# Gate stage of a hybrid Mamba-2 / S5 block: turning a group's x to tokens by VectorE block transposes and a trip through DRAM, in place of TensorE transposes

## Chip, cores and metric

One core of one Trainium2 chip runs the kernel. The metric is the device time of one execution in microseconds, lower is better.

## What is computed

The reference is a decoder block on 256 tokens with model width 2048, all in float32. One product of the normed input with `w_in` gives z, x, B, C, dt, the S5 input u and two gate vectors. The change is in the Mamba-2 mixer:

```
xbc = silu(causal_dwconv(xbc, conv_w, conv_b));  xs, bm, cm = split(xbc)
dt  = softplus(dt_raw + dt_bias)                      # (tokens, 48 heads)
xh  = xs as (tokens, 8 groups, 6 heads, 64)
y   = ssd_chunked(xh * dt_g, dt_g * a, bm, cm)        # one chunk of 256 tokens
      # cb = C B^T;  y_diag = (cb * decay) (xh * dt)
y   = (y + d_skip * xh) * silu(z); group norm; @ w_proj
```

The merged mixers then go through `w_out`, a residual, and a gated feed-forward part.

## The kernel before

Activations lie channel-major: 128 channels on the partitions, 256 tokens along the free dimension. Every weight matrix arrives in **units** of 128 x 1024 floats (512 KB). SyncE loads a unit into one of four ring slots of `raw`, ScalarE copies it to `whi` in the fp32r format (`split_hi`, L666), VectorE writes the rest `raw - whi` to `wlo` (`split_lo`, L1107), and TensorE multiplies both. Unit n's slot is loaded again once unit n has been split, and unit n+4 is split by ScalarE once TensorE has used unit n.

Each engine runs a program of its own, in the order of the code, with waits on semaphores. Nothing is scheduled by a tool: if an instruction waits, everything written behind it on that engine waits too.

The stages follow each other: u, zx (z and x, six turns), bc (B and C, two turns), gate, proj, glu, out, up, down. The **gate stage** has eight turns, one for each group of heads. Turn i multiplies the eight gate units 8i to 8i+7 (numbered 0 to 7 in the turn; I write "turn 1, unit 5") and does the attention-like part of group i between them:

- GpSimd broadcasts the decay rows of a group to all partitions, three heads a DMA (`load_decay`, L442, tile `dec`). The rows of group i+1 are asked for when TensorE's products of group i have read the buffer (`y_ready`).
- VectorE runs three scans over each half of `dec` (L1416), ScalarE takes the exponential (L853).
- TensorE computes CB = B^T C (L1924, L1925) and turns the group's three 128 x 256 tiles of x to token-major with six 128 x 128 transposes against an identity (L1933, into `XP` in PSUM). It reads copies that ScalarE has made into fixed buffers (`bst`, L856, and `xst`, L857).
- VectorE masks CB (L1428), multiplies the transposed x by dt from PSUM into `xtok` (L1433, twice), and multiplies `dec` by CB (L1422, one for each half).
- TensorE forms the heads' outputs (L1908, L1909: "heads(0)", "heads(1)").
- VectorE adds the skip term (L1478) and multiplies by silu(z) (L1481); ScalarE squares (L895); the group norm follows in the next turn.

In ScalarE's program a turn ends: split of unit 6's successor, square, the last split (`hi(7)`, which is unit 3 of the next turn), copy of the finished gate chunk out of PSUM (L899), and then the next turn's `hi(0)`, which is unit 4 of that turn. In VectorE's program turn 1 has a special order: `lo(0)` (unit 4 of turn 1), the six scans of both halves, `lo(1)` (unit 5 of turn 1), and then the mask and the decay products. In later turns the first three scans are already done at the end of the turn before. In turn 0 the heads come after all eight units, in turn 1 after unit 5, in later turns after unit 4.

Of the kernel before, what the change touches and what calls it, by code (L numbers as in the profile page):

```python
# [26 lines left out]
ds = bass.ds  # L27

P = 128
# [79 lines left out]
def build_program(nc, a, out):  # L109
    ctx = ExitStack()  # L110
    with ctx:
# [53 lines left out]
        xst = at("xst", [P, TPG, L], F32, W + 9216)  # L165
# [22 lines left out]
        bst = at("bst", [P, L], F32, C + 2048)  # L188
# [11 lines left out]
        merged_at = nc.dram_tensor("merged_blocks", (2, 4, 32, 4, 128), F32).ap()  # L200
        blocks_at = nc.dram_tensor("up_blocks", (4, 32, 4, 256), F32).ap()
# [4 lines left out]
        CB, XP = psum[:, 4, 0:ML], [psum[:, 5, 0:ML], psum[:, 6, 0:ML]]  # L206
# [7 lines left out]
        def sem(name):  # L214
# [32 lines left out]
        z_done, conv_done, xbc_done, staged, cb_ready, xp_ready, scan_ready, exp_ready, m_ready, y_ready = map(  # L247
            sem, ("z_done", "conv_done", "xbc_done", "staged", "cb_ready", "xp_ready", "scan_ready", "exp_ready",
                  "m_ready", "y_ready"))
        half_hi, half_lo = sem("half_hi"), sem("half_lo")  # L250
        ns_free, late_sum, late_h = map(sem, ("ns_free", "late_sum", "late_h"))
# [44 lines left out]
        def _(sp):  # L296
# [39 lines left out]

            for c in range(4):
# [10 lines left out]
            for name in list(PHASES)[1:]:  # L348
                groups, quads, per = PHASES[name]
                if name == "zx":  # L350

                    sp.dma_start(parm[:, KT:], a["parm"][:, KT:]).then_inc(parm_rest, 16)
                    sp.dma_start(craw[:, :, :, :], a["s5_c"]).then_inc(c_in, 16)
                if name == "up":
# [68 lines left out]
        def _(pool):  # L423
# [198 lines left out]
            with pool.Fori(0, GROUPS - 1) as i:  # L622
# [33 lines left out]
        def _(act):  # L656
# [107 lines left out]
            def group_tap(name, i, r):  # L764
# [5 lines left out]
                act.nop(nofuse=True)  # L770
                for t in range(2):
# [72 lines left out]
            def gate_turn(i, prev, last=False):  # L844
# [10 lines left out]
                def stage(g):  # L855
                    fn(bst[:, :], bc[:, ds(g, 1), 0, :].rearrange("p o n -> p (o n)"), ACTF.Copy).then_inc(staged, 1)  # L856
                    fn(xst[:, :, :], zx[:, ds(g * TPG, TPG), 1, :], ACTF.Copy).then_inc(staged, 1)  # L857

                if prev is None:
# [5 lines left out]
                    act.wait_ge(xbc_done, 16)  # L865
                    stage(0)
# [7 lines left out]
                    hi(3)  # L874
                    decay(1)
# [20 lines left out]
                hi(7)  # L896

# [201 lines left out]
        def _(dve):  # L1099
# [287 lines left out]
            with dve.Fori(1, 6) as i:  # L1387
                step.enter(i, 4 * 3 + 2 * 5, 1)
                mixer_turn("zx", i, i, ("zx", i - 1, 3))
                step.leave(6)  # L1390
            mixer_turn("bc", 0, 6, ("zx", 5, 3))
# [14 lines left out]
            def gate_turn(i, prev, first_scan=False, next_scan=True):  # L1406
# [19 lines left out]
                def tokens():  # L1426
                    dve.wait_ge(cb_ready, i + 1)
                    V.tensor_tensor(cbm[:, :], CB, mask_in[:, :], ALU.mult)  # L1428
                    dve.wait_ge(xp_ready, i + 1)
                    if prev is None:  # L1430
                        step.done(V.tensor_copy(dtt[:, :, :], DTT))
                    for k in range(2):
                        ins = V.tensor_tensor(  # L1433
                            xtok[:, k, :].rearrange("p (h n) -> p h n", h=HPG),
                            XP[k].rearrange("p (h n) -> p h n", h=HPG),
                            dtt[:, k, ds(i * HPG, HPG)].rearrange("p (h o) -> p h o", o=1).to_broadcast([P, HPG, 64]),
                            ALU.mult)
                    step.done(ins)

                if prev is None:  # L1440
# [9 lines left out]
                    tokens()  # L1450
                    blocks(0)
                    blocks(1)
                else:
# [6 lines left out]
                    tokens()  # L1460
# [8 lines left out]
                lo(4)  # L1469
                lo(5)  # L1470
# [282 lines left out]
        def _(pe):  # L1753
# [356 lines left out]
```

## Time and profile before

| what | value |
|---|---|
| median of 3 runs | 1680.87 us (1680.24 to 1680.9) |
| the profiled execution | 1680.3 us, span of its instructions 1678.6 us |
| TensorE busy | 1667.1 us, 99% |
| VectorE, ScalarE, GpSimd busy | 1320.3, 962.7, 216.4 us |
| DMA traffic | 358.49 MB, mean 214 GB/s |
| gate stage | from about 431 to 644 us of the span |

TensorE has hardly any idle time, so the time is the sum of its work as long as the other engines deliver each unit before TensorE reaches it. An engine that is less busy matters only where it hands something over late.

### The profile page before, as it was taken

The page shows a single profiled execution, that of the slowest core. Times are in us where ns is not written, and L with a number is a line of the kernel's source. Part 1 is how long each engine was busy: PE and PEld are TensorE (multiplying, and loading weights), DVE is VectorE, ACT ScalarE, POOL GpSimd, SP SyncE. Part 2 cuts the span into 40 slices and gives each one's busy share as a digit, 9 for nine tenths or more (in the row PEclk, how much of TensorE's full clock was granted, in tenths as well). Part 3 has the DMA queues.
Part 4 walks back from the last instruction along what each step waited for, and adds up shares of the span by engine and source line. Part 5 has one row for each costly group of instructions (what it writes and reads, how often), then busy time and mean ns, then how long its engine had stood idle before and what let it go on. Part 6 is the DMA issues. An engine that isn't in the chain of part 4 may idle for free.

```text
span 1678.6 us, 24422 instructions
## 1 busy us (share of the span) xinstructions
PE 1667.1 (99%) x8340; PEld 1395.1 (83%) x8340; DVE 1320.3 (79%) x1685; ACT 962.7 (57%) x1271; POOL 216.4 (13%) x310
## 2 busy tenths in 40 slices
PE   9999999999999999999999999999999999999997
PEld 8888888888788888888888888888888888888886
DVE  7999999999998986545775868888878888845555
ACT  7676676766666667444557755444444444454553
POOL 7843342221000000000000200000000000000001
PEclk9999999999999999999999999999999999999999
DMA  7666766666666566656786577777777777666653
GB/s 254 213 197 199 204 206 200 193 188 190 194 217 231 191 219 189 199 191 201 239 254 232 174 233 241 243 241 244 242 244 241 245 232 248 225 194 195 191 189 123
DMA packets 174569, 358.49 MB, mean 214 GB/s; under 512 B 16880, under 2 KB 39584, under 8 KB 174368
## 3 DMA queue, kind: packets, MB, share of 16 engines
q1 hardware_dynamic: 162528, 338.26, 62.5%
q0 software_dynamic: 11248, 18.37, 4.6%
q8 instruction: 41, 0.67, 0.2%
q10 hardware_dynamic: 720, 0.93, 0.2%
q14 instruction: 32, 0.26, 0.0%
HBM read 335.41 MB, written 15.80 MB: 209 GB/s over the span
## 4 chain that ended last, share of the span: by engine, by line
PE 73%; DVE 2%; issue 0%; ACT 0%; DVEq 0%
PE psum L1822 22%; PE psum L1823 22%; PE psum L1824 22%; PE psum L1783 3%; PE psum L1785 2%; PE psum L1908 1%; DVE wlo L1107 0%; PE psum L1909 0%; DVE vn L1749 0%; PE psum L1933 0%; DVE bc L1303 0%; PE psum L1829 0%; PE psum L1924 0%; DVE dec L1416 0%; PE psum L1982 0%; PE psum L1979 0%
## 5 line engine op out<-in xcount | busy, mean ns | idle before, releaser
L1107 DVE TENSOR_TENSOR wlo<-raw,whi 128x1024 fp32r<-128x1024 f32 x580 | 709.6, 1230 | 321.3 <-ACT whi L666 314.0
L666 ACT ACTIVATE whi<-raw 128x1024 fp32r<-128x1024 f32 x580 | 611.9, 1058 | 577.1 <-PE psum L1824 455.1
L1783 PE MATMUL psum<-act,whi 128*128 128x512 f32 x1088 | 342.5, 396 | 0.0
L1822 PE MATMUL psum<-whi,nw 128*128 128x512 f32 x704 | 274.1, 389 | 0.0
L1824 PE MATMUL psum<-whi,nw 128*128 128x512 f32 x704 | 273.9, 389 | 0.0
L1823 PE MATMUL psum<-wlo,nw 128*128 128x512 f32 x704 | 273.9, 389 | 0.0
L1785 PEld LDWEIGHTS psum<-act,wlo 128*128 128x128 f32 x1088 | 204.4, 188 | 48.3
L1785 PE MATMUL psum<-act,wlo 128*128 128x256 f32 x1088 | 213.7, 278 | 0.0
L1783 PEld LDWEIGHTS psum<-act,whi 128*128 128x128 f32 x1088 | 165.6, 189 | 3.3 <-issue 2.8
L1824 PEld LDWEIGHTS psum<-whi,nw 128*128 128x128 f32 x704 | 132.1, 188 | 27.6
L1822 PEld LDWEIGHTS psum<-whi,nw 128*128 128x128 f32 x704 | 132.1, 188 | 27.3
L1823 PEld LDWEIGHTS psum<-wlo,nw 128*128 128x128 f32 x704 | 132.1, 188 | 27.3
L1822 PE MATMUL psum<-whi,act 128*128 128x512 f32 x352 | 138.8, 394 | 0.8 <-DVE wlo L1107 0.8
L1824 PE MATMUL psum<-whi,act 128*128 128x512 f32 x352 | 137.1, 390 | 0.0
L1823 PE MATMUL psum<-wlo,act 128*128 128x512 f32 x352 | 137.1, 389 | 0.0
L1822 PE MATMUL psum<-whi,ff 128*128 128x512 f32 x264 | 102.7, 389 | 0.0
L1823 PE MATMUL psum<-wlo,ff 128*128 128x512 f32 x264 | 102.7, 389 | 0.0
L1824 PE MATMUL psum<-whi,ff 128*128 128x512 f32 x264 | 102.7, 389 | 0.0
L1822 PEld LDWEIGHTS psum<-whi,act 128*128 128x128 f32 x352 | 66.1, 188 | 16.2 <-DVE wlo L1107 1.6
L1824 PEld LDWEIGHTS psum<-whi,act 128*128 128x128 f32 x352 | 66.1, 188 | 13.9
L1823 PEld LDWEIGHTS psum<-wlo,act 128*128 128x128 f32 x352 | 66.1, 188 | 13.1
L1303 DVE SCALAR_TENSOR_TENSOR fsum<-cpad,parm,fsum 128x256 f32<-128x256 f32 x176 | 76.9, 478 | 0.0
(251 smaller groups left out, 2300.3 us busy)
## 6 DMA issues: line engine op xcount, KB each, us to landing
raw<-in_w_up SPq DMA_DIRECT2D x176, 512.0 KB, 4.9
raw<-in_w_zx SPq DMA_DIRECT2D x96, 512.0 KB, 3.7
raw<-in_w_down SPq DMA_DIRECT2D x88, 512.0 KB, 3.8
raw<-in_w_gate SPq DMA_DIRECT2D x64, 512.0 KB, 5.6
raw<-in_w_proj SPq DMA_DIRECT2D x48, 512.0 KB, 4.4
raw<-in_w_bc SPq DMA_DIRECT2D x32, 512.0 KB, 3.7
raw<-in_w_glu SPq DMA_DIRECT2D x32, 512.0 KB, 4.4
raw<-in_w_out SPq DMA_DIRECT2D x32, 512.0 KB, 4.8
```

Of the source, the lines that this page charges most:

```text
L666: fn(whi[:, s, :], raw[:, s, :], ACTF.Copy).then_inc(hi_ready, 1)
L1107: V.tensor_tensor(wlo[:, s, :], raw[:, s, :], whi[:, s, :], ALU.subtract).then_inc(lo_ready, 1)
L1303: ins = V.scalar_tensor_tensor(to[t], src, col(w, q * taps + k), to[t], ALU.mult, ALU.add)
L1783: mm(psum[:, b + t, :], whi[:, s, cols(t)], x, start=first, stop=False)
L1785: ins = mm(psum[:, b + t, L:2 * L], wlo[:, s, cols(t)], x[:, 0:L], start=False, stop=last)
L1822: mm(banks[:, t, :], x_hi, high[:, k], start=j == 0 and k == 0, stop=False)
L1823: mm(banks[:, t, :], x_hi, low[:, k], start=False, stop=False)
L1824: ins = mm(banks[:, t, :], x_lo, high[:, k], start=False, stop=last and k == 1)
L1908: mm(y, xtok[:, 0, x], dec[half][:, k, 0:L], start=True, stop=False)
```

## The change

TensorE's six transposes of x and ScalarE's two staging copies are gone; CB reads B and C where they lie. For each group, x takes another way:

1. VectorE transposes the 32 x 32 blocks of x into `xblk` (`x_turned`, two instructions of 128 x 384).
2. Four DMAs write the blocks to a DRAM buffer, 96 KB each (`token_write`), and when they have landed one DMA of 384 KB reads them back with the tokens on the partitions (`token_fetch`, tile `xraw`). For group 0 SyncE issues them during the bc stage, for the other groups GpSimd issues them from its own queue.
3. ScalarE multiplies by dt into `xtok`, one instruction of 128 x 64 for each head and each half of the tokens, 12 for a group (`tokens`). TensorE's heads wait for `xtok_ready`.

```
# GpSimd, for each i in 0..6
+                token_write(i + 1)              # waits x_blocks >= i + 2
                 for half in range(2):
                     pool.wait_ge(y_ready, i * 2 + (half + 1))
                     load_decay(i + 1, half)
+                token_fetch(i + 1)              # waits x_written, then xtok_ready
# ScalarE, gate_turn
-                def stage(g):
-                    fn(bst[:, :], bc[:, ds(g, 1), 0, :].rearrange("p o n -> p (o n)"), ACTF.Copy).then_inc(staged, 1)
-                    fn(xst[:, :, :], zx[:, ds(g * TPG, TPG), 1, :], ACTF.Copy).then_inc(staged, 1)
+                def tokens(g, k):
+                    act.wait_ge(x_read if g else first_read, 16 * max(g, 1))
+                    for hd in range(HPG):
+                        a = hd % 2 * 2
+                        ins = fn(xtok[:, k, 64 * hd:64 * hd + 64].rearrange("p (a i) -> p a i", a=2),
+                                 xraw[g][:, a:a + 2, k, hd // 2, :], ACTF.Identity,
+                                 scale=dtt[:, k, g * HPG + hd:g * HPG + hd + 1])
...
                     decay(0)
                     hi(3)
+                    act.wait_ge(dtt_ready, 1)
+                    tokens(0, 0)
+                    tokens(0, 1)
                     decay(1)
...
                 hi(5)
-                if not last:
-                    act.wait_ge(cb_ready, i + 1)
-                    act.wait_ge(xp_ready, i + 1)
-                    stage(i + 1)
                 hi(6)
...
                 hi(7)
+                if not last:
+                    tokens(i + 1, 0)
+                    tokens(i + 1, 1)
 
                 act.wait_ge(unit_used, u0 + 8)
# VectorE
+            def x_turned(g):
...
+                for k in range(2):
+                    ins = V.transpose(xblk[g][:, :, k, :, :].rearrange("p q t i -> p t q i"),
+                                      zx[:, TPG * g:TPG * g + TPG, 1, k * P:k * P + P]
+                                      .rearrange("p t (q i) -> p t q i", q=4))
+                ins.then_inc(x_blocks, 1)
+            x_turned(0)                          # before the bc stage
             mixer_turn("bc", 0, 6, ("zx", 5, 3))
...
-                            dtt[:, k, ds(i * HPG, HPG)].rearrange("p (h o) -> p h o", o=1).to_broadcast([P, HPG, 64]),
-                            ALU.mult)
...
                     if not first_scan:
                         lo(1)
+                    if i < GROUPS - 1:
+                        x_turned(i + 1)
                     lo(2)
...
                 lo(4)
+                if prev is None:
+                    x_turned(1)
                 lo(5)
# TensorE
+                    if half == 0:
+                        pe.wait_ge(xtok_ready, i + 1)
...
-                for k in range(2):
-                    for t in range(TPG):
-                        ins = nc.tensor.transpose(XP[k][:, t * P:t * P + P], xst[:, t, k * P:k * P + P], ident[:, :])
-                ins.then_inc(xp_ready, 1)
```

The loops of SyncE over the bc units and of GpSimd over the groups are written out in the changed kernel. The two places of the order that the prediction speaks of:

ScalarE, end of turn 0 and start of turn 1, in the kernel before. `whi` rows are the splits, `dec_93` and `dec_94` the two halves of the decay tile.

```order
L853 ACTIVATE dec_93<-dec_93 128x1152
L666 ACTIVATE whi<-raw 128x1024
L853 ACTIVATE dec_94<-dec_94 128x1152
L666 ACTIVATE whi<-raw 128x1024 x2
L856 ACTIVATE bst<-bc 128x256
L857 ACTIVATE xst<-zx 128x768
L666 ACTIVATE whi<-raw 128x1024
L895 ACTIVATE zx<-zx 128x3x256
L666 ACTIVATE whi<-raw 128x1024
L899 ACTIVATE gates<-psum 128x1024
L666 ACTIVATE whi<-raw 128x1024
```

The same place in the changed kernel, whose line numbers are its own (L715 is the split, L904 the exponential, L957 the gate copy):

```order
L904 ACTIVATE dec_93<-dec_93 128x1152
L715 ACTIVATE whi<-raw 128x1024
L911 ACTIVATE xtok<-xraw_103,dtt 128x64 x12
L904 ACTIVATE dec_94<-dec_94 128x1152
L715 ACTIVATE whi<-raw 128x1024 x3
L950 ACTIVATE zx<-zx 128x3x256
L715 ACTIVATE whi<-raw 128x1024
L911 ACTIVATE xtok<-xraw_104,dtt 128x64 x12
L957 ACTIVATE gates<-psum 128x1024
L715 ACTIVATE whi<-raw 128x1024
```

The two copies before `hi(6)` have gone; twelve scalings of group 0 now stand ahead of the second exponential of turn 0, and twelve of group 1, which wait for a transfer, ahead of the gate copy and of `hi(0)` of turn 1.

GpSimd's queue from the last decay loads of group 0, before. The loop body L622 to L624 runs seven times.

```order
L442 DMA dec_93<-decay_rows 128x1152
L442 DMA dec_94<-decay_rows 128x1152
L622 UNCONDITIONAL_BRANCH
L622 ISA
L442 ISA
L442 DMA dec_93<-decay_rows 128x1152
L624 REGISTER_ALU
L442 ISA
L442 DMA dec_94<-decay_rows 128x1152
L622 REGISTER_ALU
```

And in the changed kernel, for groups 1 and 2 (`token_blocks` is the DRAM buffer):

```order
L472 DMA dec_93<-decay_rows 128x1152
L472 DMA dec_94<-decay_rows 128x1152
L657 DMA token_blocks<-xblk_96 32x4x192 x4
L472 DMA dec_93<-decay_rows 128x1152
L472 DMA dec_94<-decay_rows 128x1152
L666 DMA xraw_104<-token_blocks 128x768
L657 DMA token_blocks<-xblk_97 32x4x192 x4
L472 DMA dec_93<-decay_rows 128x1152
L472 DMA dec_94<-decay_rows 128x1152
L666 DMA xraw_105<-token_blocks 128x768
```

The four writes of a group now stand ahead of its decay loads, and its fetch behind them.

## Rows read from the trace of the kernel before

**Rows 1.** The page: TensorE's busy time; its granted clock in 40 slices.
```profile
PE 1667.1 (99%) x8340; PEld 1395.1 (83%) x8340; DVE 1320.3 (79%) x1685; ACT 962.7 (57%) x1271; POOL 216.4 (13%) x310
...
PEclk9999999999999999999999999999999999999999
```

**Rows 2.** Timeline of PE, turns 5 and 6: start us, us, engine, line, tiles.
```profile
570.27 0.82 PE L1933 MATMUL psum<-ident,xst 128*128 128x128 f32 x6
...
596.18 0.82 PE L1933 MATMUL psum<-ident,xst 128*128 128x128 f32 x6
596.75 0.48 PE L1822 MATMUL psum<-whi,act 128*128 128x512 f32 x1
```

**Rows 3.** Timeline of DVE, turns 0 and 1; in brackets the idle time before, and its releaser.
```profile
454.01 0.55 DVE L1428 TENSOR_TENSOR cbm<-psum,mask_in 128x384 f32<-128x384 f32 x1
454.48 0.24 DVE L1431 COPY dtt<-psum 128x96 f32<-128x96 f32 x1
...
455.81 2.63 DVE L1422 TENSOR_TENSOR dec<-dec,cbm 128x1152 f32<-128x1152 f32 x2
...
460.63 1.25 DVE L1478 SCALAR_TENSOR_TENSOR zx<-zx,parm,psum 128x256 f32<-128x256 f32 x3
...
466.59 1.23 DVE L1107 TENSOR_TENSOR wlo<-raw,whi 128x1024 fp32r<-128x1024 f32 x1 [0.63 <-ACT whi L666]
...
472.85 1.20 DVE L1107 TENSOR_TENSOR wlo<-raw,whi 128x1024 fp32r<-128x1024 f32 x1
```

**Rows 4.** Timeline of ACT, turns 0 and 1.
```profile
453.00 1.17 ACT L853 ACTIVATE dec<-dec 128x1152 f32<-128x1152 f32 x1 [0.77 <-DVE dec L1416]
...
462.91 0.85 ACT L895 ACTIVATE zx<-zx 128x768 f32<-128x768 f32 x1 [4.85 <-DVE zx L1481]
...
464.61 1.01 ACT L899 ACTIVATE gates<-psum 128x1024 f32<-128x1024 f32 x1
465.51 1.04 ACT L666 ACTIVATE whi<-raw 128x1024 fp32r<-128x1024 f32 x1
```

**Rows 5.** Timeline of PE: the first matmul of turn 1, unit 5.
```profile
475.48 0.39 PE L1822 MATMUL psum<-whi,act 128*128 128x512 f32 x1
```

**Rows 6.** Line L722, a small copy on ACT: durations in ns, min/median/max.
```profile
L722 ACT ACTIVATE tsum<-psum x2: 271/274/276, 26.6 to 26.9; 64x128 f32<-64x128 f32 x2
```

**Rows 7.** Timeline of DVE, first turn of the bc stage.
```profile
344.57 1.22 DVE L1259 TENSOR_TENSOR rot<-psum,tab 128x1024 f32<-128x1024 f32 x1 [1.12 <-PE psum L1862]
```

**Rows 8.** Line L1536, block transposes on DVE.
```profile
L1536 DVE STREAM_TRANSPOSE turned_m<-quad_m x16: 399/418/445, 800.5 to 874.8; 128x256 f32<-128x256 f32 x16
```

**Rows 9.** Line L1433, the multiplications by dt on DVE.
```profile
L1433 DVE TENSOR_TENSOR xtok<-psum,dtt x16: 540/544/556, 454.8 to 628.3; 128x384 f32<-128x384 f32 x16
```

**Rows 10.** Line L301, 32 writes of 64 KB to DRAM, issued by SyncE.
```profile
DMA to landing us min/median/max: 2.0/3.3/4.8
```

**Rows 11.** Line L310, 8 reads of 256 KB from DRAM, issued by SyncE.
```profile
DMA to landing us min/median/max: 2.7/5.3/5.6
```

**Rows 12.** DMA issues in 443 to 640 us: engine, count, size, median us to landing.
```profile
dec<-decay_rows POOLq DMA_DIRECT2D x14, 576.0 KB, 7.4
```

**Rows 13.** All DMA of turn 3's burst, 529 to 543 us.
```profile
DMA packets 1714, 3.95 MB, mean 282 GB/s; under 512 B 112, under 2 KB 112, under 8 KB 1713
```

**Rows 14.** Timelines of ACT, DVE and PE, turns 3 and 4.
```profile
538.91 1.06 ACT L666 ACTIVATE whi<-raw 128x1024 fp32r<-128x1024 f32 x1 [3.09 <-DMA raw<-in_w_gate]
...
542.47 1.04 ACT L666 ACTIVATE whi<-raw 128x1024 fp32r<-128x1024 f32 x1
...
544.51 2.33 DVE L1107 TENSOR_TENSOR wlo<-raw,whi 128x1024 fp32r<-128x1024 f32 x2
...
553.37 1.22 DVE L1107 TENSOR_TENSOR wlo<-raw,whi 128x1024 fp32r<-128x1024 f32 x1
...
555.44 0.50 PE L1822 MATMUL psum<-whi,act 128*128 128x512 f32 x1
```

**Rows 15.** Timeline of POOL, one decay load.
```profile
461.35 0.53 POOL L442 DMA_DIRECT2D dec<-decay_rows  x1 [0.89 <-issue]
```

More of the change, by code:

```diff
@@ L164, in build_program @@
         dec = [at(f"dec{k}", [P, HALF, ML], F32, W + k * 4608) for k in range(2)]
-        xst = at("xst", [P, TPG, L], F32, W + 9216)
+        xblk = [at(f"xblk{g}", [P, 4, 2, TPG, 32], F32, off * K)
+                for g, off in enumerate((154, 140, 140, 140, 152, 152, 152, 152))]
+        xraw = [at(f"xraw{g}", [P, 4, 2, TPG, 32], F32, off)
+                for g, off in enumerate((147 * K, *[W + 9216] * (GROUPS - 1)))]
         xtok = at("xtok", [P, 2, HPG * 64], F32, W + 12288)
@@ L335, in up_fetch, with first_tokens_write, first_tokens_fetch @@
                              blocks_at.rearrange("j p q x -> (j p) (q x)")).then_inc(up_read, 16)
+            def first_tokens_write():
+                sp.wait_ge(x_blocks, 1)
+                for a in range(4):
+                    sp.dma_start(tokens_at[0, :, :, a, :].rearrange("q j x -> j q x"),
+                                 xblk[0][32 * a:32 * a + 32, :, :, :, :].rearrange("j q k t i -> j q (k t i)")
+                                 ).then_inc(first_written, 16)
+            def first_tokens_fetch():
+                sp.wait_ge(first_written, 64)
+                sp.wait_ge(cz_ready, 16)
+                sp.dma_start(xraw[0][:, :, :, :, :].rearrange("p a k t i -> p (a k t i)"),
+                             tokens_at[0].rearrange("q j a x -> (q j) (a x)")).then_inc(first_read, 16)
             for c in range(4):
@@ L353, in _ @@
                     sp.dma_start(craw[:, :, :, :], a["s5_c"]).then_inc(c_in, 16)
+                if name == "bc":
+                    for j in range(groups * quads):
+                        n = UNIT0[name] + j
+                        sp.wait_ge(lo_ready, n - RING + 1)
+                        sp.dma_start(raw[:, n % RING, :], a["w_bc"][j]).then_inc(w_in[n % RING], 16)
+                        if j == 6:
+                            first_tokens_write()
+                        if j == 24:
+                            first_tokens_fetch()
+                    continue
                 if name == "up":
@@ L621, in _, with token_write, token_fetch @@
             load_decay(0, 1)
-            with pool.Fori(0, GROUPS - 1) as i:
+            def token_write(g):
+                pool.wait_ge(x_blocks, g + 1)
+                for a in range(4):
+                    pool.dma_start(tokens_at[g % 2, :, :, a, :].rearrange("q j x -> j q x"),
+                                   xblk[g][32 * a:32 * a + 32, :, :, :, :].rearrange("j q k t i -> j q (k t i)")
+                                   ).then_inc(x_written, 16)
+            def token_fetch(g):
+                pool.wait_ge(x_written, 64 * g)
+                if g > 1:
+                    pool.wait_ge(xtok_ready, g)
+                pool.dma_start(xraw[g][:, :, :, :, :].rearrange("p a k t i -> p (a k t i)"),
+                               tokens_at[g % 2].rearrange("q j a x -> (q j) (a x)")).then_inc(x_read, 16)
+            for i in range(GROUPS - 1):
+                token_write(i + 1)
                 for half in range(2):
@@ L770, in group_tap @@
                 act.nop(nofuse=True)
+                if name == "bc" and i == 0 and r == 1:
+                    act.wait_ge(first_written, 64)
                 for t in range(2):
@@ L864, in gate_turn @@
                     act.wait_ge(y5_ready, 8)
-                    act.wait_ge(xbc_done, 16)
-                    stage(0)
                     group_tap("bc", 1, 3)
@@ L1449, in gate_turn @@
                     lo(3)
-                    tokens()
+                    mask_cb()
                     blocks(0)
@@ L1459, in gate_turn @@
                         lo(1)
-                    tokens()
+                    mask_cb()
                     blocks(0)
```

40 lines of the change are left out of this document (23 added, 17 removed).

## The prediction

> **What bounds the kernel now.** I read the page first. TensorE is busy for 99% of the span at a granted clock that never leaves its upper level, 2.4 GHz [rows 1]. So every microsecond of TensorE work that goes is a microsecond of time, but only while the others keep their appointments with it. Then I read the timelines of the gate stage, engine by engine, to see how early each unit is ready. The reader is to see there that the appointments are tight in two places. In turn 1 VectorE itself waits 0.63 us for ScalarE's split of unit 4, `hi(0)`, which ends at 465.51 + 1.04 = 466.55. It then works without a pause through six scans to `lo(1)`, done at 472.85 + 1.20 = 474.05 [rows 3, 4]. TensorE starts on that unit 5 at 475.48 [rows 5]: 1.4 us of slack behind `hi(0)` of turn 1, and no more. In turn 4 the same unit is ready at 553.37 + 1.22 = 554.59 and used at 555.44, a slack of 0.85 [rows 14].
>
> **What the change takes away.** On TensorE six transposes go in each of eight turns. Their busy time says 0.82 us, but matmuls overlap: the next unit starts 596.75 - 596.18 = 0.57 us after the first of them [rows 2]. So 0.57 x 8 = 4.6 us could be won. ScalarE loses two copies a turn that stand ahead of a split which mostly waits for its weights anyway (3.09 us in turn 3 [rows 14]); I cost that at nothing. VectorE loses two multiplications, 2 x 0.54 = 1.1 us a turn [rows 9]. CB keeps its products.
>
> **What it adds.** VectorE: two block transposes of 128 x 384. The nearest row is 418 ns for 256 columns [rows 8], so at most 1.5 x 418 = 627 for 384 and at least 418; I take 0.56, 1.1 us for a group. That cancels against the multiplications. Group 0's pair falls just ahead of a place where VectorE waited 1.12 us for TensorE [rows 7], which covers it; without that cover it would cost up to 1.1 us at the stall of turn 0. SyncE's five DMAs for group 0 lie ahead of weight loads that are wanted some units later; nothing. ScalarE: 12 scalings of 128 x 64 a group. A copy of 64 x 128 takes 0.274 us [rows 6]. Half the columns cost between half of that and all of it, 0.14 to 0.27; a fixed part is likely, so I take 0.25, that is 3.0 us a group (1.6 to 3.3). GpSimd's queue: five more DMAs a group, four of them ahead of the decay loads at 0.53 us each [rows 15]. DMA: 0.39 MB written and 0.39 MB read back for each group.
>
> **The handover to turn 1, step by step**, in times of the trace of before. Turn 0: dt's tokens leave PSUM first, about 454.0 + 0.24 = 454.3 [rows 3]. Group 0's scalings run until 457.3, so the second exponential, which began at 453.00 [rows 4], ends at 457.3 + 1.1 = 458.4. VectorE's second decay product follows it, half of the 2.63 us of both [rows 3]: 459.8. Then a split of 1.2, 461.0; the transposes, 462.1; the next split, 463.2; the skip term and the product with silu(z), which took from 460.63 to 462.91 with the handover, 2.3: 465.5 [rows 3, 4]. ScalarE squares and makes its last split, another 1.7 (462.91 to 464.61 [rows 4]): 467.2, where it comes to `tokens(1, 0)` and waits for the fetch.
>
> GpSimd meanwhile: blocks ready 462.1; four writes issued until 464.2, and the last, issued at 463.7, lands 3.3 us later by the 64 KB writes [rows 10], at 467.0. The decay loads are issued meanwhile, behind the writes. The fetch is issued at 467.1. Its landing: 256 KB took 2.7 at best and 5.3 in the median [rows 11], 576 KB behind such traffic 7.4 [rows 12]. It is of 384 KB and queues behind two decay loads and three units, so I take 6.2: 473.3. Then 3.0 of scaling, 0.9 for the gate copy (464.61 to 465.51) and 1.04 for `hi(0)` [rows 4]: 478.2 instead of 466.55, 11.7 us later. Behind the waiting instruction stand the gate copy, `hi(0)` and both exponentials of turn 1, and VectorE's `lo(0)`, scans and `lo(1)` wait for those. Less the 1.4 us of slack, turn 1's unit 5 starts 11.7 - 1.4 = **10.3 us later** than before. Turn 0's and turn 1's own 0.57 are inside this, since the chain no longer runs through TensorE. Bounds: fetch 2.7 and scalings 1.6 give 469.8 + 1.6 + 1.9 = 473.3, 5.4 later; fetch 7.4 and 3.3 give 479.7, 11.8 later.
>
> The Trainium skill, page "DMA: Bandwidth & Descriptors", section "Anatomy of one DMA — SWDGE (gpsimd) path", gives a DMA about 2.0 us plus its bytes at 436 GB/s. For the fetch that would be 2.9 us (an estimate from the page), and turn 1 would come only 7.0 us later. The decay loads of this trace do not agree: by the page 3.4, measured 7.4 [rows 12], so I stay with the rows.
>
> **The later handovers**, turns 1 to 2 up to 6 to 7, six of them. A turn lasts 596.18 - 570.27 = 25.9 us [rows 2]; TensorE alone needs 25.3 without the transposes. The loop over the other engines is 25.9 - 0.85 = 25.05 long [rows 14]. Twelve scalings push `hi(0)` from 543.5 by 3.0. VectorE started that split, the second of the pair at 544.51, only at about 545.6 [rows 14], so 2.1 of it were free, and the two multiplications that it drops give back 1.0. That leaves the loop at 25.05 plus L, the time by which weights or the fetch arrive late because 0.79 MB join the burst. At the burst's 282 GB/s [rows 13] that is 2.8 us at most, 0 if it falls into gaps. The writes and the fetch precede only part of what ScalarE waits for, so I take L = 1.0. Then a turn lasts 26.05, 0.15 more than before, and six of them add 0.9. Each microsecond of L above 0.25 costs 6.
>
> **Sum.** 10.3 + 0.9 = 11.2. The profiled execution took 1680.3 (span 1678.6 and 1.7 around it), 0.6 below the median, so 1691.5 for such an execution and 1692.1 against the median of 1680.9.
>
> **Rivals.**
> *Later turns free.* L is under 0.25: six turns give back 0.57 each, 3.4 in all. 10.3 - 3.4 = 6.9, 1687.8. For it: ScalarE has idle time in every turn and bursts have gaps. Against: ScalarE waits for weights in that burst today [rows 14].
> *Later turns held.* L = 2: 6 x 1.15 = 6.9, with 10.3 that is 17.2, 1698.1. For it: the fetch is issued behind writes, their landing and both decay loads.
> *The clock falls.* Unit 4 of turn 1 would be wanted one unit ahead of 475.48, near 472.7, and be ready at 478.2 + 1.2 = 479.4; unit 5 would be ready at 485.8. TensorE would stand idle for some 6.7 us and then 3.6. Before, the granted clock stayed at 2.4 GHz, but no wait in it was that long, so the rows do not say. A unit takes at most 25.3 / 8 = 3.2 us; at 1.2 GHz it would take twice that. Unit 4's excess is hidden in the wait for unit 5, one more slow unit would add about 3: 1695. The page "TensorE: Matmul & The Clock Gate" of the Trainium skill, Part 1, says that activity releases the throttle and idling brings the lower level back, which is this case.
> *The handover is hidden (faster).* Everything turns on `hi(0)` of turn 1. If it were at most 1.4 us late, nothing would stall and 4.6 would be won: 1676.3. Up to 1.4 + 3.4 = 4.8 us late the change still breaks even (L = 0). For it: the fetch may be quick, and my turn-0 chain may be too long. Against: the scalings alone are 1.6 or more, and even the best row for the fetch leaves `hi(0)` 6.8 us late.
> *No measurable change.* The lower bound of turn 1, 5.4, less 3.4 is 2.0, 1682.9. It needs both at once.
>
> **Chances.** Forecast 0.46, later turns free 0.18, held 0.14, clock 0.10, hidden 0.05, no change 0.07. A difference of 0.2%, 3.4 us, is about what a measurement of this kernel can tell from none. Faster 0.05, same 0.07, slower 0.88. The range: from 1684.5, between the two low cases, to 1700, above "held", where bounds of fetch (1.4 more) and of L come together.
>
> **What the profile after would show.** Right: ScalarE waits several microseconds for the DMA of `xraw` ahead of the first scaling of group 1; TensorE has about 10 us of idle time in turn 1, released by VectorE's `wlo`; the scalings last about 0.25 each; block transposes about 0.56; later turns lie 26 us apart. Wrong: no wait on `xraw`, or TensorE still without idle time in turn 1 (then the fetch is quick, and the time falls); turns 25.3 apart (L is nothing) or over 27 (L is larger); a granted clock under 1.0 in turn 1; waits of TensorE on `xtok` itself, which I do not expect, as `hi(0)` stands behind the scalings and is missed first.

## The result and the profile after

The changed kernel took 1711.94 us in the median of 4 runs (1710.56 to 1713.45), the kernel before 1680.74 beside it (4 runs, 1680.24 to 1680.9). The ratio is 1.0186, with a 95% interval of 1.0169 to 1.0204. The forecast was 1692.1 in a range up to 1700.0: the sign was right, the size was not. The profiled execution has a span of 1711.5 us against 1678.6, 32.9 more. It was the slowest of the four, 1.5 us above their median, so the 32.9 us that are divided up below are 1.7 us more than the difference of the medians, 31.2.

The page of the changed kernel: busy times, which answer to [rows 1], and, from its fourth part, the chain of work that ended last, by engine.

```profile
PE 1670.2 (98%) x8292; PEld 1391.9 (81%) x8292; DVE 1320.9 (77%) x1685; ACT 978.0 (57%) x1351; POOL 235.7 (14%) x345
...
PE 61%; DVE 5%; DMA 5%; ACT 3%; issue 1%; POOL 0%; DVEq 0%; ACTq 0%
```

TensorE has 48 matmuls fewer and yet 3.1 us more of busy time, so part of its work ran slower. The chain has 5% of the span, some 85 us, on DMA; before, the same line named PE with 73%, DVE with 2% and no DMA. These shares say through what the chain runs, not how much was lost there.

Where do the 32.9 us lie? TensorE begins CB at the same place of every turn, so its first and last start in a window tell how long the turns are. First the kernel before, then the changed one, each in 458 to 700 us (turns 1 to 7) and 480 to 700 us (turns 2 to 7): line, durations in ns, first and last start.

```profile
L1924 PE MATMUL psum<-bc,bst x14: 377/378/378, 466.0 to 622.1; 128*128 128x256 f32 x14
...
L1924 PE MATMUL psum<-bc,bst x12: 377/378/378, 491.9 to 622.1; 128*128 128x256 f32 x12
```

```profile
L2002 PE MATMUL psum<-bc x14: 377/378/379, 467.3 to 650.3; 128*128 128x256 f32 x14
...
L2002 PE MATMUL psum<-bc x12: 377/378/378, 505.4 to 650.3; 128*128 128x256 f32 x12
```

Turn 1 begins 1.3 us late. From turn 1 to turn 2 it takes 38.1 us instead of 25.9: 12.2 more. The five turns after that take (650.3 - 505.4) / 5 = 28.98 us each instead of 26.04: 14.7 more. What is left, 4.7, comes behind the start of turn 7, nearly all of it inside that turn: its unit 5 already begins 32.6 us later than before. So the first handover cost 13.5 and the six later ones 14.7 + 4.7 = 19.4.

Turn 1 in the changed kernel, engine by engine: ACT, DVE and PE, which answer to [rows 4], [rows 3] and [rows 5].

```profile
475.87 2.97 ACT L911 ACTIVATE xtok<-xraw,dtt 128x64 f32<-128x64 f32 x12 [9.25 <-DMA xraw<-token_blocks]
478.75 1.00 ACT L957 ACTIVATE gates<-psum 128x1024 f32<-128x1024 f32 x1
479.65 1.04 ACT L715 ACTIVATE whi<-raw 128x1024 fp32r<-128x1024 f32 x1
```

```profile
480.73 1.22 DVE L1165 TENSOR_TENSOR wlo<-raw,whi 128x1024 fp32r<-128x1024 f32 x1 [12.85 <-ACT whi L715]
481.87 5.20 DVE L1491 TENSOR_TENSOR_SCAN dec<-dec,mask 128x384 f32<-128x384 f32 x6
486.98 1.20 DVE L1165 TENSOR_TENSOR wlo<-raw,whi 128x1024 fp32r<-128x1024 f32 x1
```

```profile
482.01 0.79 PE L1893 MATMUL psum<-whi,act 128*128 128x512 f32 x1 [8.39 <-DVE wlo L1165]
488.24 0.50 PE L1893 MATMUL psum<-whi,act 128*128 128x512 f32 x1 [1.66 <-DVE wlo L1165]
```

Read downwards, this is the chain of the prediction: ScalarE waits 9.25 us for the fetch, then come scalings, gate copy and `hi(0)`; VectorE, idle for 12.85 us, splits and scans; TensorE waits 8.39 us at unit 4 and 1.66 at unit 5. That unit starts at 488.24, 12.8 us later than before.

The waits of the gate stage, 440 to 700 us: engine, line and tile that waited, what ended it, us in total, times, longest.

```profile
DVE wlo L1165 <- ACT whi L715: 55.1, 24, 12.8
ACT whi L715 <- DMA raw<-in_w_gate: 24.9, 10, 4.1
...
PEld psum L1981 <- ACT rs L726: 16.4, 6, 2.9
...
ACT xtok L911 <- DMA xraw<-token_blocks: 13.4, 5, 9.2
```

The third row is nearly new, before it had 0.4 us: ahead of the heads of turns 2 to 7 TensorE waits six times for `rs`, ScalarE's logarithm of the group norm. The ACT and PE rows of turn 3 show why it is late:

```profile
544.28 1.17 ACT L904 ACTIVATE dec<-dec 128x1152 f32<-128x1152 f32 x1 [1.86 <-DVE dec L1491]
545.46 1.28 ACT L726 ACT_TABLE_LOAD   x1
546.75 0.38 ACT L726 ACTIVATE rs<-psum 128x256 f32<-128x256 f32 x1
```

```profile
547.19 1.13 PE L1981 MATMUL psum<-dec,xtok 128*64 128x256 f32 x4 [2.44 <-ACT rs L726]
```

VectorE's scans end late, the second exponential waits for them, behind it stand a table load and the logarithm, and only then are the heads allowed to write, since the norm's sum lies in their PSUM bank (PSUM is the memory of TensorE's results; the kernel uses it as eight banks).

### The profile page after: what moved, and what is told of

It reads as the page before. It is cut to its first block, busy times and chain, and to the rows that moved or that the text cites. A ratio compares the mean times of both kernels' runs of the same rounds, so it can differ in the third digit from the quotient of the medians.

```text
span 1711.5 us, 24289 instructions
## 1 busy us (share of the span) xinstructions
PE 1670.2 (98%) x8292; PEld 1391.9 (81%) x8292; DVE 1320.9 (77%) x1685; ACT 978.0 (57%) x1351; POOL 235.7 (14%) x345
## 2 busy tenths in 40 slices
DMA packets 177194, 364.78 MB, mean 213 GB/s; under 512 B 17521, under 2 KB 41185, under 8 KB 176993
## 4 chain that ended last, share of the span: by engine, by line
PE 61%; DVE 5%; DMA 5%; ACT 3%; issue 1%; POOL 0%; DVEq 0%; ACTq 0%
PE psum L1893 19%; PE psum L1895 18%; PE psum L1894 18%; PE psum L1854 3%; DMA xraw<-token_blocks 2%; DVE wlo L1165 2%; PE psum L1856 2%; DVE dec L1491 1%; DMA token_blocks<-xblk 1%; ACT xtok L911 1%; DMA raw<-in_w_gate 1%; DVE dec L1497 1%; ACT whi L715 1%; POOL token_blocks L657 0%; ACT gates L957 0%
## 5 line engine op out<-in xcount | busy, mean ns | idle before, releaser
L715 ACT ACTIVATE whi<-raw 128x1024 fp32r<-128x1024 f32 x580 | 611.8, 1058 | 584.2 <-PE psum L1895 458.6
L1893 PEld LDWEIGHTS psum<-whi,nw 128*128 128x128 f32 x704 | 132.1, 188 | 27.5
L1894 PEld LDWEIGHTS psum<-wlo,nw 128*128 128x128 f32 x704 | 132.1, 188 | 27.3
```

Source lines behind the costliest of these rows:

```text
L715: fn(whi[:, s, :], raw[:, s, :], ACTF.Copy).then_inc(hi_ready, 1)
L1893: mm(banks[:, t, :], x_hi, high[:, k], start=j == 0 and k == 0, stop=False)
L1894: mm(banks[:, t, :], x_hi, low[:, k], start=False, stop=False)
```

## Experiments

Times are medians, each beside runs of the kernel before on the same chip (1680.2 to 1680.7). "1 to 2" is the time between the starts of CB in turns 1 and 2, "later turn" the mean of the five intervals between turns 2 and 7, both read as above. These two columns come from one execution of each kernel: e9 and e11 have the same order in the gate stage and differ by 0.22 us in the last column, so differences of a few tenths there say little.

| kernel | median us | against before, 95% | 1 to 2 | later turn |
|---|---|---|---|---|
| before | 1680.7 | | 25.9 | 26.04 |
| changed | 1711.9 | 1.0169 to 1.0204 | 38.1 | 28.98 |
| e1_order | 1692.2 | 1.0052 to 1.0085 | 31.3 | 26.74 |
| e2_ns_bank | 1711.7 | 1.0168 to 1.0202 | 38.1 | 28.42 |
| e3_static_x | 1699.6 | 1.0099 to 1.0132 | 29.8 | 27.98 |
| e4_no_transfers | 1684.8 | 1.0014 to 1.0034 | 29.2 | 25.78 |
| e5_writes_only | 1696.0 | 1.0078 to 1.0112 | 29.7 | 27.92 |
| e6_filler | 1709.3 | 1.0152 to 1.0186 | 39.1 | 28.60 |
| e7_early | 1685.4 | 1.0017 to 1.0036 | 30.1 | 26.22 |
| e8_early_ns | 1683.7 | 1.0008 to 1.0027 | 31.6 | 25.46 |
| e9_early_turn1 | 1679.7 | 0.9988 to 1.0006 | 25.3 | 25.66 |
| e10_static_writes_late | 1694.2 | 1.0064 to 1.0095 | 29.7 | 27.06 |
| e11_late_sum | 1679.25 | 0.9981 to 0.9999 | 25.3 | 25.88 |
| e12_third_early | 1679.7 | 0.9987 to 1.0005 | 25.3 | 25.60 |

### Order alone: e1_order

```
                     hi(1)
+                    tokens(i, 0)
+                    tokens(i, 1)
                     decay(1)
...
                 hi(7)
-                if not last:
-                    tokens(i + 1, 0)
-                    tokens(i + 1, 1)
```

> Order alone: the scalings of group i (i >= 1) stand in turn i behind the split of unit 5, ahead of the second exponential, instead of at the end of turn i-1 ahead of the gate copy. The same scalings, transposes and transfers. Theory (ScalarE's order: the wait for the fetch and the 3 us of scalings stand ahead of hi(0) and all that follows it): unit 5 of turn 1 starts near 476 instead of 488.2, but the wait for the fetch (to about 476) and the scalings now hold the second exponential, so the head products of turn 1 start some 4 us later than before, and 8 to 9 of the 12.8 us come back; in later turns the scalings fall into the idle time ahead of the second exponential and 1 to 2.5 us a turn come back. In all 1711.9 - 9 - 12 = about 1691 (1685 to 1698). Rival (the transfers themselves, 0.79 MB a turn, make weights and decay rows late): the later turns stay near 29 us, about 1703. Rival (the fallen clock is what costs in the later turns): it returns only if the idle time goes; the granted clock shows which.

(In turn 6 the gate copy also waits for the last writes, which had landed.) Measured: 1692.2, 19.7 us less. The interval from turn 1 to turn 2 gave back 6.8 us of it. The scalings stand in turn 4 where ScalarE used to wait for the scans, and the second exponential follows without a pause:

```profile
554.42 1.04 ACT L715 ACTIVATE whi<-raw 128x1024 fp32r<-128x1024 f32 x1
555.36 2.96 ACT L911 ACTIVATE xtok<-xraw,dtt 128x64 f32<-128x64 f32 x12
558.23 1.15 ACT L904 ACTIVATE dec<-dec 128x1152 f32<-128x1152 f32 x1
```

The transfers are all still there, so the rival that they alone make the later turns late falls for 2.24 of the 2.94 us a turn. ScalarE even waits longer for its gate weights here than in the changed kernel:

```profile
ACT whi L715 <- DMA raw<-in_w_gate: 36.3, 13, 5.0
```

I read this so: late weights cost less where no scalings stand behind them.

### The norm's bank: e2_ns_bank

```
-                root(TPG * P, yrs_ready, g + 2)
+                root(TPG * P, yrs_ready, g + 2, YNS)     # psum[:, 6, 0:L]
...
-                if prev is not None:
-                    pe.wait_ge(ns_free, i + 1)
                 heads(0)
```

> The group norm's sum gets a PSUM bank of its own (bank 6), so the head products no longer wait for ScalarE's Ln; nothing else changes. Theory (late scans are carried over the second exponential, the table load and the Ln to the head products): heads start when the first decay product is ready, some 1.3 us earlier in each of six or seven turns, 1711.9 - 8 = 1704 (1700 to 1708). Rival (late weights and fetches set the turn): the turn stays 29 us and the time within 2 us of 1712.

Measured: 1711.7, no change. The theory missed here. TensorE's wait ahead of the heads only got another releaser, VectorE's decay product, and shrank from 2.44 to 1.35 us in turn 3; the rest of the loop was as late as before. The mean later turn fell by 0.56 in the traces, but the changed kernel's trace is of its slowest run and this one of its fastest; the medians differ by 0.2. A wait that is seen on the engine in question is not yet what sets the time.

### No wait for the fetch, no transfers, writes only: e3, e4, e5

```
# e3: tokens(g, k)
-                    act.wait_ge(x_read if g else first_read, 16 * max(g, 1))
+                    if g in (0, GROUPS - 1):
+                        act.wait_ge(x_read if g else first_read, 16 * max(g, 1))
...
-                                 xraw[g][:, a:a + 2, k, hd // 2, :], ACTF.Identity,
+                                 (a view of mask of the same shape if g else xraw[0][...]), ACTF.Identity,
# e4: GpSimd, besides
-                token_write(i + 1)
-                token_fetch(i + 1)
# (VectorE's wait for the writes goes too; of ScalarE's waits only that for group 0 stays)
# e5: only token_fetch(i + 1) goes; ScalarE waits as in e4
```

All three leave out the true x of groups 1 to 6 (e4 and e5 of group 7 as well), so their y is wrong and only their times count.

> The scalings of groups 1 to 6 read a tile that is always there (the mask) and don't wait for the fetch; group 7's still waits; all transfers, transposes and scalings run. Leaves out: the y of groups 1 to 6 is computed from wrong x. Theory (ScalarE's order): the wait of 9.3 us ahead of turn 1 goes, the 3.0 us of scalings stay: unit 5 of turn 1 starts about 8.7 us earlier; the later waits for the fetch (some 4 us together) go too: 1711.9 - 8.7 - 4 = 1699 (1695 to 1703). Rival (transfers delay weights and decay rows): turn 1 gains the same, the later turns stay: 1703. Rival (the number of ScalarE's scalings is the main cost in turn 1): only 5 or so come back.

> As the run with the mask read in place of x, and the writes and fetches of groups 1 to 7 are gone as well; transposes and scalings stay, group 0 keeps its transfers. Leaves out: x of groups 1 to 7 isn't moved. Rival (transfers): what it gains over the run with transfers is what they cost the weights and decay rows: 2 us a turn, 12 in all, down to about 1687. Theory (ScalarE's order and the Ln): less than 1 us a turn, 1693 to 1699.

> As the run without transfers (1684.8), but the four writes of blocks to DRAM stay for groups 1 to 7; the fetches are gone. Leaves out: the x of groups 1 to 6 and 7 is the mask, as there. The run with writes and fetches took 1699.6, so 14.8 us hang on the transfers. The writes stand in GpSimd's queue ahead of both decay loads and take their 2.3 us of issue there, and they land ahead of the turn's burst of weights. Theory (position: what stands ahead of the decay loads and the burst costs, what comes behind costs little): the writes bring back 9 to 13 of the 14.8 us, 1694 to 1698. Rival (bytes: both move 0.39 MB, each costs its half): 1691 to 1693. Rival (the fetch is what costs): 1685 to 1688.

Measured: 1699.6, 1684.8 and 1696.0. The first is what the theory said: without the wait for x, 12.4 us come back, 8.3 of them between turns 1 and 2. The second is the rival's number and beyond it: with the scalings where the change put them but without the transfers, a later turn takes 25.78 us, 0.26 less than before, though 0.5 more than the 25.3 that TensorE needs. So twelve scalings by themselves cost the later turns at most that half microsecond, and the transfers, with the wait for them away in groups 1 to 6, cost 14.8 us. With the writes alone 11.2 of these are there, more than their half of the bytes. But e3 still waits for group 7's fetch, and e4 and e5 don't. The later turns of e3 and e5 are alike (27.98 and 27.92); what parts them comes in turn 7, where ScalarE waits for that fetch in e3 (0.40 us) and TensorE then waits 2.44 us ahead of the heads, against 0.27 in e5. What the fetches cost by their bytes alone is not shown.

How do they cost it? By the burst I mean the stretch of a turn in which gate weights and decay rows are under way together. The DMA issues of 500 to 650 us: engine, count, size, median us from issue to landing; the kernel before first, then e4, then the changed kernel.

```profile
raw<-in_w_gate SPq DMA_DIRECT2D x39, 512.0 KB, 5.9
dec<-decay_rows POOLq DMA_DIRECT2D x10, 576.0 KB, 7.7
```

```profile
raw<-in_w_gate SPq DMA_DIRECT2D x41, 512.0 KB, 4.8
```

```profile
raw<-in_w_gate SPq DMA_DIRECT2D x41, 512.0 KB, 7.0
dec<-decay_rows POOLq DMA_DIRECT2D x10, 576.0 KB, 7.6
xraw<-token_blocks POOLq DMA_DIRECT2D x6, 384.0 KB, 7.4
```

The weights take 2.2 us longer in the median than in e4, and 1.1 longer than in the kernel before; the decay rows take no longer than before, but are issued behind the writes. This agrees with the Trainium skill, page "DMA: Bandwidth & Descriptors", section "Issuing engines are not separate DMA queues": transfers of SyncE and GpSimd run on the same 16 DMA engines and interleave, whoever issues them.

### The clock: e6_filler

```
+                if i == 1:
+                    for _ in range(40):
+                        mm(WARM, ones[:, :], ones[:, :], start=True, stop=True)
                 unit_tokens("gate", i, 4, act16)
+                if i > 1:
+                    for _ in range(10):
+                        mm(WARM, ones[:, :], ones[:, :], start=True, stop=True)
```

> The changed kernel with matmuls of ones into an unused PSUM bank while TensorE would wait: 40 ahead of unit 4 of turn 1 (a wait of 8.4 us), 10 ahead of the head products of turns 2 to 7 (waits of 1.9 to 2.4 us). They add no dependence. Theory (in later turns the fallen clock is a cost of its own, 1.7 us in every second turn, and 3.4 in turn 1): the granted clock stays at its upper level through the gate stage, and 5 to 8.5 us come back, 1703.4 to 1707. Rival (the other engines set the pace, TensorE's slow stretch is hidden in its next wait): the clock stays up and the time moves by less than 2 us, 1710 to 1713. If the fillers are longer than the waits they add up to 5 us.

Measured: 1709.3, 2.6 less, between the two. Stretches of the gate stage, the changed kernel and then this one: us, TensorE busy, granted clock, DMA share, GB/s.

```profile
466.00:490.00 24.00, 13.83 (x53) 0.86 0.49 160
505.00:533.00 28.00, 24.62 (x123) 1.00 0.65 212
533.00:562.00 29.00, 25.60 (x121) 0.94 0.64 217
```

```profile
466.00:490.00 24.00, 20.95 (x133) 1.00 0.48 158
490.00:494.00 4.00, 4.00 (x18) 0.57 0.35 120
505.00:533.00 28.00, 27.48 (x146) 1.00 0.64 210
533.00:562.00 29.00, 28.80 (x151) 1.00 0.68 231
```

The clock stays at 2.4 GHz through the fillers and unit 4, and the handover doesn't get shorter (39.1 against 38.1; the fillers took 9.1 us there, 0.7 more than the wait they were to fill). TensorE merely waits longer for unit 5, 2.94 us instead of 1.66, and starts it at 488.75 instead of 488.24. The clock isn't up for the whole stage, though: it fell behind that wait, from 490.2 to 493.6. In e2 the slow stretch of turn 1 lasted 10.2 us, in the changed kernel 6.8, and unit 5 starts at 488.24 in both. So in turn 1 the fallen clock was hidden in the next wait.

In the later turns its price is less certain. Turns 3 and 5 of the changed kernel, in which it fell, are long, 30.5 and 30.4 us, but 27.5 and 27.3 follow them. The fillers give 28.60 in the mean instead of 28.98, and 2.6 us in all, less what they cost themselves. In e2's trace the clock never fell in turns 2 to 7, and its median is that of the changed kernel. Between nothing and some 3 us is what these runs allow.

In the later turns of the changed kernel the clock fell at 546.8, 604.9 and 662.9, in turns 3, 5 and 7, each time within 0.4 us of the end of a wait of 2.44 us.

### Is it the order in GpSimd's queue? e10_static_writes_late

```
# on top of e3
             for i in range(GROUPS - 1):
-                token_write(i + 1)
                 for half in range(2):
                     pool.wait_ge(y_ready, i * 2 + (half + 1))
                     load_decay(i + 1, half)
+                token_write(i + 1)
                 token_fetch(i + 1)
```

> As the run with the mask read in place of x (1699.6, all transfers kept), but GpSimd issues both decay loads ahead of the four writes instead of behind. Leaves out: as there. Same bytes in the same burst. Theory (the writes cost through what they stand ahead of: 2.2 us of issue and their landing ahead of the decay loads): the decay rows land 2 to 3 us earlier and 5 to 9 of the 14.8 us that the transfers cost go: 1691 to 1695. Rival (the bytes are in the burst either way, and the weights behind them come as late): 1698 to 1701.

Measured: 1694.2, 5.4 of the 14.8 us, with the same bytes in the same burst. Decay rows landed 7.0 us after issue instead of 7.5, weights 5.5 instead of 6.7. So at least a third of the transfers' cost was their place ahead of the decay loads. Of the 9.4 us that are left not all can be put to their being in the burst: this kernel waits for group 7's fetch, which e4 doesn't, and longer than e3, since the writes are now issued later:

```profile
ACT xtok L912 <- DMA xraw<-token_blocks: 3.2, 1, 3.2
```

### Moved out of the way: e7, e8, e9

```
# e7, on top of e1. GpSimd:
+                if i:
+                    pool.wait_ge(exp_ready, 2 * i + 1)
                 token_write(i + 1)
+                if i:
+                    token_fetch(i + 1)
                 (both decay loads)
-                token_fetch(i + 1)
+                if i == 0:
+                    token_fetch(1)
# VectorE: x_turned(i + 2) ahead of lo(7) of turn i, not x_turned(i + 1) behind lo(1)
# (in turn 0 x_turned(1) behind blocks(1))
# ScalarE, turn 0: decay(1) ahead of tokens(0, .)
# e8: e7 with the bank of e2
# e9, on top of e8: x_turned(1) beside x_turned(0), written by SyncE, fetched by GpSimd at the
# start of turn 0; tokens(1, .) ahead of decay(0) of turn 1; x_turned(2) behind blocks(1) of turn 1
```

> Scalings behind the split of unit 5, and the moves a turn earlier: group g's block transposes at the end of turn g-2 on VectorE, its writes in turn g-1 once the first exponential is done, its fetch behind them ahead of the next decay loads; in turn 0 the second exponential ahead of the scalings. The same instructions and bytes as the changed kernel. Theory (ScalarE's order and the traffic in the burst are the whole loss): the later turns come down to 25.3 to 25.6 us, turn 1 to within 3 us of before: 1677 to 1682. Rival (bytes count wherever they are moved): later turns of 26.5 or more, over 1687.

> As the run before it, and the group norm's sum in a PSUM bank of its own, so that the head products don't wait for ScalarE's Ln behind scalings and second exponential. Alone on the changed kernel it gave nothing. Theory (it gave nothing since late weights held the turn; with these on time the Ln behind the scalings is next): 1 to 3 us less than the run without it. Rival (TensorE itself sets the turn then): within 1 us of it.

> The run with early moves and the norm's own bank (1683.7), changed at the handover to turn 1 alone, where 34.0 us were left against 28.4 before: group 1's blocks are transposed and written beside group 0's in the mixer stage and fetched at the start of turn 0, its scalings stand ahead of turn 1's first exponential, in 6.1 us of ScalarE's idle time; group 2's blocks are transposed in turn 1, in VectorE's 3 us of idle time, not at the end of turn 0 behind a wait of 2.1 us. The same number of transposes, scalings and bytes. Theory (the moves and scalings cost only where they stand on the chain between the engines): turn 1 comes to about 28, later turns stay at 25.3, and 5 to 6 us go: 1678 (1676 to 1680), faster than before by 2. Rival (12 scalings a group are too much for ScalarE in turn 1 wherever they stand): turn 1 over 31, 1681 or more.

Measured: 1685.4, 1683.7 and 1679.7. The first missed: later turns of 26.22 were not yet 25.6, and "1 to 2" stayed 4.2 above before. The bank that had been worth nothing alone was now worth 1.7 us, and brought the later turns to 25.46; "1 to 2" was even longer, 31.6, with a slow clock from 485.0 to 488.4. It then came down to 25.3 in the third, 0.6 less than before, which is what six transposes were worth. In all the third gained 4.0 us, where 5 to 6 were expected. TensorE's waits for VectorE in the whole gate stage are two rows in that kernel:

```profile
PE psum L1910 <- DVE wlo L1179: 1.6, 2, 1.4
PE psum L1917 <- DVE zx L1572: 0.7, 1, 0.7
```

TensorE, VectorE and ScalarE run as many instructions as in the changed kernel and the same 364.78 MB are moved; places in the order, the norm's bank, a buffer and the engine that issues group 1's writes differ, and 32.2 us are gone. The fetch, issued in a quieter stretch of a turn, lands in 3.4 us in the median (e7, 500 to 650 us) where the changed kernel needed 7.4:

```profile
xraw<-token_blocks POOLq DMA_DIRECT2D x5, 384.0 KB, 3.4
```

During two of these fetches (533.0 to 536.5 and 559.0 to 562.5) the DMA engines were busy to 0.60 and 0.61, during three of the changed kernel's (from 499.6, 527.3 and 556.9, 7.1 to 7.4 us each) all the time.

### Last steps: e11, e12

```
# e11, on top of e9
-                    if c == 0 and j == 0:
+                    if c == 0 and j == 1:
                         group_squares(GROUPS - 1)
# e12, on top of e11: x_turned(2) behind blocks(1) of turn 0; token_write(2), token_fetch(2)
# behind turn 1's decay loads (i == 0), not behind turn 2's
```

> The run with turn 1 mended (1679.7), and TensorE's sum for the last group's norm behind unit 1 of the projection instead of behind unit 0. In that run unit 1 of the projection ended 4.15 us after unit 0, before 3.19: TensorE arrives there ahead of VectorE and waits 1.0 us. Theory (what is won on TensorE in the gate stage is lost again at the next appointment): 1.0 us less, 1678.7. Rival (the wait only moves to the next unit or to the projection's tail): no change.

> As the run before it, and group 2's block transposes in turn 0, its writes behind turn 1's decay loads and its fetch behind the scalings of turn 1, instead of all of it in the burst of turn 1. Turns 2 and 3 took 25.71 and 26.29 us, the others 25.28: 1.4 us to win if that burst made them late. Theory (traffic in the burst): both come to 25.3 to 25.5, 1.0 to 1.4 us less than the run before it, about 1677.4. Rival (they are late for other reasons, or the writes now delay turn 1's decay rows): within 0.5 us of it, or turn 1 over 28.

Measured: 1679.25 and 1679.7. e11 was to win 1.0 us over e9. By the medians it won 0.5, and 0.2 if each is taken against the runs of the kernel before beside it (1680.43 and 1680.69), so its gain over e9 is not shown. Its ratio to before is 0.999, 0.9981 to 0.9999: about 1 us, too little to be called a gain with confidence. e12 missed the 1.0 to 1.4 us that it was to win, and gained nothing in the median, though its profiled execution was the quickest of all (1677.6, span 1675.6). Its 11 runs spread over 4.4 us (1677.6 to 1682.0), 21 runs of the kernel before over 2.3. Why the versions with more transfers scatter more was not tried. A gain of 4.6 us on TensorE was there to take, and no version took more than about a fourth of it in the median. In e9 turn 7 begins 2.4 us earlier than before (619.5 against 621.9); where the rest stayed was not traced.

## Why the prediction was right in sign and wrong in size

**The handover to turn 1: right in its chain, 2.5 us short.** Forecast 10.3, measured 12.8 at unit 5. Scalings 2.97 us (3.0 forecast), `hi(0)` done at 480.69 (478.2). The step that was short is the fetch: it was issued at 469.14 instead of 467.1, since the last write ahead of it landed 5 us after its issue and not 3.3, and took 6.7 instead of 6.2. Without the wait for it, e3 gave back 8.3 us. The scalings last 0.333 us each, not 0.25, but each begins 0.24 us behind the one before, so the sum of 3.0 for twelve held.

**What was costed at nothing or little: right.** Block transposes lasted 0.553 us each (0.56 forecast). Group 0's transposes ahead of the bc stage did not delay the gate stage: turn 0's CB begins at 444.0 in both kernels. Turn 1 begins 1.3 us late for the chain in turn 0: with the second exponential ahead of group 0's scalings (e7), turn 0 takes 21.6 us instead of 23.3. TensorE's own 25.3 us a turn was right too; e8 has four intervals of 25.28.

**The later handovers: "L = 1.0" failed.** The forecast was 26.05 us a turn; it was 28.98. By the prediction's sum, 25.05 plus L, L was 3.9 and not 1.0. The sum has two parts, and the runs part them. "2.1 of it were free, and the two multiplications that it drops give back 1.0" held nearly: in e4 the scalings stand in place and a turn takes 25.78, where 25.3 would follow. "The writes and the fetch precede only part of what ScalarE waits for, so I take L = 1.0" was wrong: 28.98 - 25.78 = 3.2 us, and 3.0 by the medians (27.2 us between the two kernels, less 8.9 between turns 1 and 2, over six handovers). That is above even its bound of 2.8.

What was overlooked in the step? First, the bound counted bytes at the burst's rate, but the writes also stood in GpSimd's queue ahead of both decay loads (e10: at least a third of the cost). The prediction lists their issue time and puts none of it into L. Second, as I read the runs, the slack was spent twice. The scalings used up what ScalarE had between its weights and VectorE's need; the transfers then delayed the weights, with little left to absorb it. Each alone is cheap: scalings without transfers 25.78 a turn, transfers with scalings out of the way 26.74 (e1), though ScalarE waited 36.3 us for weights there and 24.9 in the changed kernel. Together they make 28.98, from 26.04 before. Counted from the 25.3 that TensorE needs, that is 0.5, 1.4 and 3.7 us. That both in place cost more than the two together is measured; that it is this slack which they share is the reading that fits, and no run leaves the scalings out altogether. "Each microsecond of L above 0.25 costs 6" held: 2.94 x 6 is 17.6, and the later handovers cost 19.4 more than before.

**The signs.** Two of those that were named as wrong showed: turns over 27 us, and a granted clock under 1.0 in turn 1. No wait of TensorE on `xtok` did, as forecast. The wait for `rs` ahead of the heads was not foreseen, 13.8 us of TensorE in six turns, but e2 shows that it did not set the time.

**Rivals.** "Later turns held" had the right mechanism with L = 2, too small. "The clock falls" came true as an event, 1.2 GHz from 478.6 to 485.4, and had hardly a price in turn 1; it fell in later turns too, where I had not looked for it, and e6 gives 2.6 us for what it kept away. What it costs is decided by whether TensorE waits again behind the slow stretch. The Trainium skill's page "TensorE: Matmul & The Clock Gate", Part 1, named in the prediction, is borne out in turn 1: the clock fell in the wait of 8.39 us, at 478.6, and came back at 485.4, while unit 4 ran. "The handover is hidden" named the right place: with `hi(0)` on time, turn 1 takes 25.3.

**The price of the fetch.** The prediction put the 2.9 us that it had worked out from the Trainium skill's page "DMA: Bandwidth & Descriptors" aside for the rows of the decay loads. For the changed kernel that was right: 6.7 to 7.9, median 7.1. In e7 the shortest was 3.2, close to that estimate. In the burst the same transfer took at least twice as long.

## What to carry to other kernels

When two edits draw on the same slack, add their costs before comparing with it: instructions on the engine that receives data and transfers that make the data late are not two small terms here. Count for a DMA what stands behind it in its queue and in the burst, and look for the stretch of the turn in which the DMA engines are less busy. The transfers cost 15 us where the change had put them; with all moves earlier a later turn takes 25.66 us (e9), where TensorE alone needs 25.3. Before removing a wait that the profile shows, ask what ends next to it: the norm's bank was worth nothing in the changed kernel, and 1.7 us once the scalings and the transfers were out of the way.

## What the runs showed of the hardware

- In the later turns of the changed kernel TensorE waits 1.9 to 2.4 us ahead of the heads, after steady work. Near the end of three of these waits, all of 2.44 us, the granted clock fell to its lower level, 1.2 GHz (0.94 in the mean of the stretches around turns 3 and 5); near the same wait of turn 2, and near those of 2.15 and 1.91 us in turns 4 and 6, it did not. So it fell not only at long waits, and not each time.
- A 128 x 64 scaling on ScalarE with a pointer for its factor lasts 333 ns and begins 0.24 us behind the one before (12 in 2.97). The Trainium skill's page "ScalarE: Activation LUTs", section "What ACT_TABLE_LOAD costs", gives figures from which this form comes to about 332 ns (an estimate: 186 + 93 for one pointer + 0.833 x 64) and an overlap of 93: the trace agrees.
- The same 384 KB fetch took 3.2 us at best (e7) and 7.9 at worst (the changed kernel). In windows around single fetches the DMA engines were busy to 0.60 and 0.61 in e7, and to 1.0 in three of the changed kernel's.
